# A hybrid decoder step: the first eight K pages asked for earlier, and every later page request tied to the landing of the page four before it

## What is computed

```python
def gather(pool, j):
    rows = pool[j][page_table]                    # (8, 32) pages of 128 x 12 x 64
    return rows.reshape((dec_b, past) + rows.shape[3:])

def fox_sample(k_past, v_past, logf_past, q, k, v, logf):
    ...
    suffix = (lax.cumsum(lp, axis=1, reverse=True) - lp).transpose(0, 2, 1)
    g = jnp.cumsum(logf.astype(F32), axis=1).transpose(0, 2, 1)
    s_past = einsum('bqhd,bkhd->bhqk', q, k_past) * scale + g[..., :, None] + suffix[..., None, :]
    s_new = einsum('bqhd,bkhd->bhqk', q, k) * scale + g[..., :, None] - g[..., None, :]   # causal
    p = softmax(concatenate([s_past, s_new], axis=-1))
    return einsum(p[..., :n_past], v_past) + einsum(p[..., n_past:], v)
```

## Time and profile before

| | us |
|---|---|
| median of 3 runs | 2198.92 |
| lowest, highest | 2190.67, 2200.44 |
| the profiled execution | 2196.55 |
| its span in the trace | 2194.8 |

### The profile page before, as it was taken

The page is one execution under the profiler, slowest core; times in us unless marked ns, Lnnn a source line. Parts: engine busy times, 40 slices in busy tenths (PEclk is TensorE's granted clock), DMA queues, the critical chain, the costliest instruction groups (busy, mean ns, idle before and its releaser), DMA issues.

```text
span 2194.8 us, 39552 instructions
## 1 busy us (share of the span) xinstructions
PE 1990.1 (91%) x16059; PEld 1473.1 (67%) x16059; DVE 1047.0 (48%) x1915; ACT 345.6 (16%) x828; POOL 192.4 (9%) x228
## 2 busy tenths in 40 slices
PE   6999588888988677899999998999998899999996
PEld 3778354555555345677777776777776677777774
DVE  5442576666776654533344443304364533344453
ACT  2002122222222111122210001111011122210002
POOL 1400000000000001100002222000001000012220
PEclk9999798999999889999999999999898999999998
DMA  4110698999999994122222223121111122222211
GB/s 169 61 55 4 237 360 317 344 328 357 334 366 350 334 399 173 48 77 77 77 77 77 77 77 115 39 77 39 63 60 49 39 77 78 77 81 81 81 64 43
DMA packets 127602, 320.32 MB, mean 146 GB/s; under 512 B 9852, under 2 KB 10130, under 8 KB 127294
## 3 DMA queue, kind: packets, MB, share of 16 engines
q1 hardware_dynamic: 123874, 304.65, 38.3%
q0 software_dynamic: 3296, 12.98, 1.7%
q10 hardware_dynamic: 252, 0.16, 0.0%
HBM read 309.20 MB, written 8.55 MB: 145 GB/s over the span
## 4 chain that ended last, share of the span: by engine, by line
PE 85%; DVE 4%; issue 4%; DMA 3%; SPq 2%; ACT 1%; ACTq 0%; POOL 0%; DVEq 0%
PE ps L827 51%; PE ps L1005 5%; PE ps L1036 3%; PE ps L1135 3%; PE ps L1136 3%; PE ps L742 1%; PE ps L970 1%; PE ps L743 1%; DMA work<-in_cache_k 1%; PE ps L958 1%; PE ps L959 1%; PE ps L771 1%; PE ps L982 1%; PE ps L772 1%; DMA wring<-in_cache_v 1%
## 5 line engine op out<-in xcount | busy, mean ns | idle before, releaser
L827 PE MATMUL ps<-work 128*128 128x288 f32 x1152 | 296.5, 411 | 12.3 <-DVE work L1636 7.8
L827 PE MATMUL ps<-xn,wring 128*128 128x288 f32 x1008 | 268.8, 410 | 16.7 <-DVE xn L1589 15.7
L827 PEld LDWEIGHTS ps<-work 128*128 128x128 f32 x1152 | 221.6, 193 | 75.5 <-issue 13.6
L827 PE MATMUL ps<-big,wring 128*128 128x288 f32 x944 | 251.5, 410 | 7.6 <-DVE big L2137 7.6
L1853 DVE STREAM_TRANSPOSE work<-work 128x768 f32<-128x768 f32 x256 | 234.5, 954 | 27.1 <-DMA work<-in_cache_k 27.0
L827 PEld LDWEIGHTS ps<-xn,wring 128*128 128x128 f32 x1008 | 193.3, 192 | 71.8 <-issue 16.5
L827 PEld LDWEIGHTS ps<-big,wring 128*128 128x128 f32 x944 | 181.0, 192 | 58.8 <-DVE big L2137 8.5
L1005 PE MATMUL ps<-work,big 32*32 32x256 f32 x6144 | 146.2, 399 | 57.0 <-issue 47.2
L1663 DVE TENSOR_TENSOR work<-ps,work 128x288 f32<-128x288 f32 x72 | 32.9, 458 | 320.8 <-PE ps L827 320.8
L675 POOL TENSOR_TENSOR h<-h,xn 128x288 f32<-128x288 f32 x96 | 106.0, 1106 | 812.5 <-DVE xn L1670 697.7
L1005 PEld LDWEIGHTS ps<-work,big 32*32 32x32 f32 x6144 | 91.6, 105 | 99.3 <-issue 63.6
(11 more groups left out here) (354 smaller groups left out, 2410.4 us busy)
## 6 DMA issues: line engine op xcount, KB each, us to landing
work<-in_cache_k SPq DMA_DIRECT2D x256, 384.0 KB, 7.3
wring<-in_cache_v SPq DMA_DIRECT2D x256, 384.0 KB, 6.2
wring<-in_w_up SPq DMA_DIRECT2D x16, 2048.0 KB, 9.1
wring<-in_w_down SPq DMA_DIRECT2D x16, 2048.0 KB, 7.8
wring<-in_w_in_odd SPq DMA_DIRECT2D x6, 2048.0 KB, 8.0
wring<-in_w_in_even SPq DMA_DIRECT2D x5, 2048.0 KB, 7.9
wring<-in_w_out_odd SPq DMA_DIRECT2D x2, 2048.0 KB, 8.0
big<-in_x_prompt SPq DMA_DIRECT2D x1, 2048.0 KB, 8.8
```

The source lines that it names most:

```text
L827: last = mm(bank, w[:, k, :], x[:, k, :], start=k == 0 and not onto, stop=k == 3, skip_group_check=onto)
```

## The change

SP's first wait is now for the end of the `sfxT` products instead of the end of the `sfx` copies; the latter wait stands before K page 8. `stage_queries(0)` and the transposes of pages 0 to 7 move ahead of the K row copies in DVE's order. POOL lays group 0's bias before it stores K rows. PE's wait for `v_stored` moves to SP, before the last block of output weights. `turn_new(0)`, `weigh_new(0)` on PE and `take_new(0)`, `start_out(0)` on DVE move behind group 0's scores and maximum. And in SP's loop each V request n waits for the landing of K page n+12, each K request n+16 for the landing of V page n: in SP's order that is in both cases the request four before.

```diff
@@ SP @@
             sp.wait_ge(sem("ptab_in"), 16)
-            wait_emptied(sp, FIRST["sfx"] + 6)
+            sp.wait_ge(block_in, FIRST["sfxT"] + H)
...
+            def k_landed(n):
+                sp.wait_ge(k_in[n % KSLOTS], 16 * (n // KSLOTS + 1))
+
+            def v_landed(n):
+                sp.wait_ge(v_in[n % VSLOTS], 16 * (n // VSLOTS + 1))
+
             for n in range(0, KSLOTS, 4):
                 ids = page_ids(n)
+                if n == GP:
+                    wait_emptied(sp, FIRST["sfx"] + 6)
                 for m in range(4):
                     k_page(n + m, ids[m])
             for n in range(0, NB * PAGES - KSLOTS, 4):
                 v_ids, k_ids = page_ids(n), page_ids(n + KSLOTS)
                 for m in range(4):
+                    k_landed(n + KSLOTS - 4 + m)
                     v_page(n + m, v_ids[m])
                 for m in range(4):
+                    v_landed(n + m)
                     k_page(n + KSLOTS + m, k_ids[m])
...
             sp.wait_ge(sem("scored"), NG)
+            sp.wait_ge(sem("v_stored"), 32)
             unit("out0", 1)
@@ POOL @@
+            wait_emptied(pool, FIRST["sfx"] + 6)
+            own(pool.memset(bias_nat, 0.0))
+            lay_bias(0)
             kp = O["k_prompt"][0, 0].rearrange("(t p) h d -> t p (h d)", p=P)
...
-            pool.wait_ge(block_in, FIRST["pooled"] + 2)
-            own(pool.memset(bias_nat, 0.0))
-            for g in range(NG):
-                if g:
-                    pool.wait_ge(sem("bias_turned"), g)
...
+            for g in range(1, NG):
+                pool.wait_ge(sem("bias_turned"), g)
+                lay_bias(g)
@@ PE @@
-            pe.wait_ge(sem("v_stored"), 32)
...
             score_new(0)
-            turn_new(0)
-            weigh_new(0)
             for g in range(NG):
...
                 add_bias(g)
+                if g == 0:
+                    turn_new(0)
+                    weigh_new(0)
@@ DVE @@
+            stage_queries(0)
+            turn_pages(0, range(GP))
             rows("knat", lambda t: kstage[:, t, :])
...
-            stage_queries(0)
+            turn_bias(0)
             shift_new(0)
-            take_new(0)
-            start_out(0)
-            turn_bias(0)
-            turn_pages(0, range(GP))
             for g in range(NG):
...
                 shift_group(g)
+                if g == 0:
+                    take_new(0)
+                    start_out(0)
```

More of the change, by code:

```diff
@@ L637, in _, with lay_bias @@
                 .then_inc(sem("stored"), 16)
+            def lay_bias(g):
+                lo = g * GP * H
+                pool.tensor_copy(bias_nat[:, :, 0:H],
+                                 sfx[:, lo:lo + GP * H].rearrange("p (n h) -> p n h", h=H))\
+                    .then_inc(sem("bias_laid"), 1)
+            wait_emptied(pool, FIRST["sfx"] + 6)
+            own(pool.memset(bias_nat, 0.0))
+            lay_bias(0)
             kp = O["k_prompt"][0, 0].rearrange("(t p) h d -> t p (h d)", p=P)
@@ L1796, in rows, with stage_queries, turn_page, turn_pages @@
                     cp(d[0:r, 512:FOX], bankB(s, FOX - 512, r)).then_inc(out_of["vector"], 1)
+            def stage_queries(b):
+                if b >= 2:
+                    dve.wait_ge(sem("scored"), GS * (b - 1))
+                src = q4.rearrange("p (c i f) t -> p i c f t", c=CG, i=HC)
+                for i in range(HC):
+                    ins = cp(qcur[:, b % 2, :, i, :, NS * i:NS * i + NS], src[:, i, :, :, NS * b:NS * b + NS])
+                ins.then_inc(sem("queries_staged"), 1)
+            def turn_page(n):
+                slot = n % KSLOTS
+                dve.wait_ge(k_in[slot], 16 * (n // KSLOTS + 1))
+                x = k_ring[:, slot, :]
+                nc.vector.transpose(x, x).then_inc(sem("k_turned"), 1)
+            def turn_pages(g, pages):
+                if g < NG:
+                    for p in pages:
+                        turn_page(g * GP + p)
+            stage_queries(0)
+            turn_pages(0, range(GP))
             rows("knat", lambda t: kstage[:, t, :])
@@ L1837, in head_out @@
                 cp(big[r, EV_Q + hd // 2, 0:SEQ], ps[r, 2, :]).then_inc(sem("fox_prompt_done"), 1)
[L1839 to L1853, removed]
             def turn_bias(g):
```

## The result

The changed kernel takes 2296.61 us (median of 4 runs, 2292.48 to 2301.48). The kernel before took 2194.8 us beside it (4 runs, 2184.3 to 2200.44). The ratio is 1.0466, 95% interval 1.043 to 1.0502: slower, 38.6 us more than the 2258 us that were forecast, and inside the range of 2200 to 2305, near its upper end. The profiled execution of the changed kernel took 2298.19 us, its span is 2296.4.

A forecast was written before the change was run, and what follows sets the result against it. The page stage was taken to run close to the sixteen DMA engines' limit, alternating with compute. Opening -20.9, rounds +86.1 and tail -4 gave +61 us on 2196.55, so 2258 us; range 2200 to 2305, leaving out 2 in 10.

The forecast's parts named there:

- the likeliest case: Whole kernel: page-stage rounds of 9.8 to 11.1 us, giving 2217 to 2293 us; chance 65%.
- The round: SP's page loop: eight pages take 10.5 us instead of 9.04, adding 86.1 us over 59 rounds.
- the term for the burst: SP's page loop: 7.2 us from a burst's first request to its last landing, the mean of seven bursts.
- that floor: SP's page loop: a round with the waits takes at the very least 9.25 us, 0.15 + 3.2 + 5.9.
- The opening: Start of the page stage: earlier K pages and moved work let group 0 be scored at 247.9, 20.9 us sooner.
- Cover: 2 us: Opening: DVE finishes turning K0 to K7 near 226, before the first K row copy at 228.06; lateness beyond delays PE.
- the opening doesn't come: Rival, opening: K7 lands after 228 or V0 waits long; group 0 gains 10 us, not 21: 2268; no chance given.
- The tail: End of the page stage: the last sixteen V requests start behind four pages rather than eight or nine, -4 us.
- Clean rounds: Rival, page loop: bursts land in under 6.3 us, rounds of 9.25 to 9.5 us, 2183 to 2199; chance 17%.
- Compute on top: Rival, page loop: slow groups' waits add to rounds, +0.5 us each, 2288; 18% shared with worse bursts, 2285 to 2330.
- worse bursts: Page loop: bursts landing later than assumed, 2285 to 2330 us; 18% shared with compute on top.
- Other signs: Page stage: V and K bursts spread over 3 to 4 us, DMA share near 0.75, K252's request near 867 us.

The follow-up runs named there:

- e2: Kernel before with only the two landing waits in SP's loop added: 2313.24 us, ratio 1.053.
- e10: Changed kernel with every round's eight page numbers read twice, four pages under way: 2455.51 us, ratio 1.1164.
- e7: Changed kernel with page numbers read once before the loop, every round fetching the same eight pages, four under way: 2213.65 us, ratio 1.005.
- e3: Changed kernel with the next round's page numbers read between a burst's requests, four pages under way: 2250.08 us, ratio 1.0242.
- e1: Changed kernel without the two landing waits in SP's loop, new opening kept: 2179.49 us, ratio 0.9921.
- e11: Changed kernel without landing waits, requesting half of each page once the slots have been filled: 2109.02 us, ratio 0.9588.
- e5: Changed kernel without landing waits, with the next round's page numbers read between a burst's requests: 2179.91 us, ratio 0.99.
- e6: Changed kernel with eight pages under way instead of four: 2183.12 us, ratio 0.9927.
- e4: Changed kernel with six pages under way instead of four: 2190.53 us, ratio 0.9985.
- e8: Changed kernel, limit of four kept, requesting half of each page once the slots have been filled: 2163.77 us, ratio 0.983.
- e9: Changed kernel with five pages under way instead of four: 2233.49 us, ratio 1.0154.

## Why the prediction came out right, point by point

**The direction and its mechanism held.** The waits bite from the first full round, the loop becomes the bound, and compute hides behind it: after the change SP has no wait for a scored group in 651 us. e2 shows that the waits alone do it, and e10 that more reading comes back whole: +2.8 us a round for 2.7 us of reading. The size was forecast too small: +61 us, where the spans differ by 101.6. Of the 40.6 us that are missing the rounds are 31.9, the opening 5.2 and the tail 2.8, which leaves 0.7. All three errors go the same way, and the time of 2296.6 us lies above the 2217 to 2293 us that stood for the likeliest case. The direction was no luck, but the range held by little more than 8 us.

**The round: 10.5 us predicted, 11.04 measured.** The chain was 0.15 (landing to K request) + 3.2 (to the next V request) + 7.2 (to the fourth landing). The trace has 0.16 + 3.37 + 7.56, means over the rounds, 11.09 together. The largest miss is the term for the burst. The mean of 7.2 is that of seven bursts. In the changed kernel 58 of 59 V bursts start with one or two pages under way. The trace before has 20 bursts in 268 to 806 us that start with two or fewer, and their mean from first request to last landing is 7.6 us; with it the sum would have been 0.15 + 3.2 + 7.6 = 10.95 us. Such a burst lands unevenly. In the changed kernel the first page of a V burst is in 3.16 us after its request, the next three 1.47, 1.90 and 1.03 us behind each other, where 0.96 is the rate of full queues. With four under way each of these delays stands in the round. 10.55 was also rounded to 10.5. Over 59 rounds it is 59 x 0.54 = 31.9 us.

**The cause was told too narrowly.** The prediction put the loss on the 3.2 us of reading that drain the engines and took 9.25 us as the least that a round could be; that floor used the lone page's 3.0 us and 0.96 a page. e7 shows that even with no reading the limit of four costs 9.64 us a round. Of the 2.0 us that the round grew, 0.6 are lost by the number under way alone (9.64 against 9.04) and 1.4 by the reading on top (11.04 against 9.64). e3's expectation, 8.8 to 9.7 us a round, took the reading as wholly hidden. e7, without any, comes to 9.64 and inside it, so e3 with its 10.25 missed by the reading that still stood inside its bursts.

The Trainium skill, "DMA: Bandwidth & Descriptors", section "Anatomy of one DMA — SWDGE (gpsimd) path", fits a transfer that GpSimd issues as 2.0 us plus bytes at 436 GB/s, an estimate of 2.9 us for a page. The page gives it for that path alone, and these pages are asked for by SP. The trace agrees for a page that lands first (3.0 before, 3.16 in the bursts under the limit) and not for one of four under way (4.8 us in e7), and it is the second that the loop pays. By the fit the change would have been some 30 us faster; the measurement is 102 us slower.

**The opening: -20.9 us predicted, -15.7 measured.** By the prediction's own two times it is 268.71 - 247.9 = 20.8. Group 0's scores end at 252.94 instead of 247.9. The chain of waits after the change, with the pieces that were not in the sum (start us, us, what):

```profile
214.66 2.07 PE ps L922 x2
216.73 1.45 PE ps L923 x2
...
246.42 3.12 issue
249.53 2.20 PE ps L1019 x43
251.73 1.21 PE ps L1027 x8
```

Two pieces are missing from the forecast. The first products of the suffix sums took 2.07 and 1.45 us where the later ones of the same chain take 0.86: the granted clock was 0.72 in 214 to 220 us, as the second stretch above shows. That pushes the K row copies from 228.06 to 230.06:

```profile
220.52 7.81 DVE L1827 STREAM_TRANSPOSE work<-work 128x768 f32<-128x768 f32 x8 [2.75 <-DMA work<-in_cache_k]
230.06 0.69 DVE L1810 COPY wring<-ps 128x512 f32<-128x512 f32 x1 [1.74 <-PE ps L944]
```

DVE's eight transposes were done at 228.33, 1.74 us before the first copy could start. The second piece is a wait of PE inside group 0's scores that has no releaser in the profile, 3.12 us. By all signs PE waits there for its own instructions (last section). The bias, with 1.21 us instead of 0.69, adds 0.5.

The cover of 2 us named in the prediction ("Cover: 2 us") was used up to the last. K0 to K7 took 4.7 to 6.5 us to land and not 3 to 5, and in e1, where the granted clock was 1.00, the chain goes through K1's landing and DVE's eight transposes:

```profile
215.97 5.40 DMA work<-in_cache_k
221.39 3.89 DVE work L1825 x4
225.29 2.89 DVE work L1825 x3
228.18 0.69 DVE wring L1808
```

The first copy starts at 228.18, 0.1 us later than before the change. The rival "the opening doesn't come" had K7's landing after 228 as its condition; K7 landed at 227.3 and that rival stayed off by 0.7 us.

**The tail: -4 us predicted, -1.2 measured.** The last V requests are spread out by SP's waits for slots that PE still uses, so the number of pages ahead of them counts for little (start us, us, what):

```profile
918.69 14.45 SPq L523 DMA_DIRECT2D wring<-in_cache_v  x8
```

One of these waits, for the V products at L1050, lasts 7.1 us.

**The rivals and the signs.** Clean rounds did not come: no round mean of any kernel with a limit of four and whole pages is below 9.64. Compute on top did not come either; "worse bursts", which shared its 18%, came in part. The forecast "ten to eleven us from one V burst to the next with nothing waiting on scores" is what the timeline shows, at its upper end. Other signs were off. From the first to the fourth request V bursts took a mean 2.0 us and not 3 to 4, since only the K requests wait, and K bursts 4.4. K252 went at 904.4 and not near 867. DMA's share was 0.84 and not near 0.75; the forecast's own round gives 0.95 x 9.04 / 10.5 = 0.82.

## What to carry to other kernels

A limit on transfers under way costs at least (landing time with that many under way) / (their number) for each transfer, and the landing time to put in is the one measured under load, 4.8 us here, not the 3.0 us of a lone transfer: at 0.96 us a page this stage needed six to eight 384 KB pages under way. What the requesting engine does between seeing a landing and asking for the next page then adds to it. With four under way the first 2.7 us of reading cost 1.4 us a round, because a part of it lay beside landings, and a second 2.7 us cost 2.8; without a limit the reading cost nothing. Of a change with two halves, measure each half alone: here 0.8% of gain lay under 5.3% of loss.

## What the runs showed that was not expected

**PE's waits without a releaser follow the number of pages under way, and they end when instructions have come in.** The score products and the V products wait for nothing that the profile names. The groups at these two over 253 to 780 us: e1 (no limit, DMA share 0.95), then e7 (four under way, 0.95), then e11 (half pages, no limit, 0.64).

```profile
PE ps L1017 <- issue: 37.2, 18, 3.5
PE ps L1048 <- issue: 16.8, 8, 3.1
```

```profile
PE ps L1019 <- issue: 22.8, 14, 2.7
...
PE ps L1050 <- issue: 4.1, 4, 1.7
```

```profile
PE ps L1019 <- issue: 12.2, 11, 2.9
...
PE ps L1050 <- issue: 1.3, 2, 0.7
```

54.0, 26.9 and 13.5 us. The DMA share does not order them: e1 and e7 have the same. What does is how many pages are under way, and how large they are. For each group of eight pages these waits are 1.8 to 2.1 us without a limit or with eight or six under way (e1, e5, e6, e4), 1.6 with five, 0.9 to 1.1 with four, whether the share is 0.95 (e7), 0.93 (e3), 0.84 (the change) or 0.67 (e10), and 0.4 with half pages (e8, e11).

What PE waits for stands in the list of DMA queues of the changed kernel's page (packets, MB, share):

```profile
q8 instruction: 129, 2.11, 0.4%
```

These are packets of 16 KB. In 253 to 780 us the changed kernel has 59 of them for 15,039 matmuls and weight loads of PE, and e1 70 for 17,837: one packet for 255 in both. All 13 waits without a releaser of the changed kernel in this stretch end 1.25 to 1.67 us after such a packet has come in; a moment picked at random lies 1.2 to 1.8 us behind one in 7% of cases. The wait of 3.12 us in the opening does the same (packet in at 248.02, PE on at 249.53), and so do 28 of 34 waits in e1. So PE waits there, by all signs, for its own instructions. It is read from times and counts; no run changed the number or the place of these packets. A packet takes about 1.0 us at every limit, so the longer waits lie in what comes before it starts. That it queues behind the pages fits, but when it is asked for the trace does not show.

**The granted clock in the opening.** With the K pages requested early, seven of eleven profiled executions (the changed kernel, e3, e6, e8, e9, e10, e11) show a granted clock of 0.72 to 0.74 in 214 to 220 us, and four (e1, e4, e5, e7) show 1.00; the two kernels with the old opening show 1.00. 2.4 GHz is 1.00, and in the stretch the engine was at 1.2 GHz for a part of it. In the changed kernel PE had been 100% busy with transposes in 208 to 214 us at 1.00. Without the dip K16 goes at 248.6 to 252.0 us, with it at 252.1 to 253.6. The dip itself costs 1.8 us by the chain above (2.07 + 1.45 against 2 x 0.86); the rest of that difference is the wait for instructions in group 0's scores, which is 1.4 to 1.8 us in e1, e4 and e5 and 2.5 to 4.0 in all others, e7 among them. The landing waits are not the cause of the dip, since kernels of both kinds are in both groups. What is the cause is open.

**A page's landing where the opening's stores run.** K0's request at 215.8 took 4.7 us to land, and 4.9 us in e1, though no page was under way when it was made, against 3.0 for such a page of the stage and 3.0 for K0 itself in the kernel before. The stores of the log gates have just been issued there; whether they are what it waits behind was not tried. Where the 1.7 us between a page's first and last engine come from stays open as well.
